# The first two column blocks of each up projection as a fourth group of seven block products, with weight sums added up in DRAM

## What is computed

```python
def squared_relu_mlp(u, w_up, w_down):        # u 512 x 1024, w_up 1024 x 4096, w_down 4096 x 1024
    return jnp.square(jax.nn.relu(u @ w_up)) @ w_down
...
    # layer 0, before its MLP: the chunked scan
    X = (xh * dt[..., None]);  dA = dt * A;  cs = jnp.cumsum(dA, axis=2)
    seg = cs[:, :, :, None] - cs[:, :, None, :]
    Lmat = jnp.exp(jnp.where(causal, seg, -jnp.inf))
    y_diag = jnp.einsum("bclsgr,bcsgrp->bclgrp", CB[..., None] * Lmat, X)
```

## Time and profile before

| | us |
|---|---|
| Median of 3 runs (1261.75 to 1262.09) | 1261.78 |
| Span of the profiled execution, first to last instruction | 1260.5 |
| PE busy | 1252.7 |
| DVE busy | 923.8 |
| ACT busy | 754.1 |
| POOL busy | 168.1 |

### The profile page before, as it was taken

How to read it: one execution, slowest core, us unless ns; L and a number is a source line. 1 busy time by engine, 2 the same in 40 slices (tenths; PEclk the granted TensorE clock), 3 DMA queues, 4 the chain that set the end, 5 groups by cost and what they waited for, 6 DMA issues and landing times.

```text
span 1260.5 us, 19569 instructions
## 1 busy us (share of the span) xinstructions
PE 1252.7 (99%) x7651; PEld 1087.3 (86%) x7651; DVE 923.8 (73%) x1261; ACT 754.1 (60%) x1277; POOL 168.1 (13%) x197
## 2 busy tenths in 40 slices
PE   9999999999999999999999999999999999999998
PEld 8788888888888989999888898788889999988886
DVE  5676786898743686687887974877576776869886
ACT  6655455687653655567565753777554566666563
POOL 0046355473000000000000000000000000000000
PEclk9999999999999999999999999999999999999999
DMA  8488878385663378668676527656626576877554
GB/s 273 154 285 275 237 169 198 111 238 123 176 217 105 128 173 235 216 113 218 190 249 191 193 74 171 131 125 154 169 96 235 113 198 226 174 221 239 188 175 155
DMA packets 110530, 230.29 MB, mean 183 GB/s; under 512 B 8150, under 2 KB 18918, under 8 KB 110182
## 3 DMA queue, kind: packets, MB, share of 16 engines
q1 hardware_dynamic: 84384, 159.93, 38.8%
q0 software_dynamic: 21760, 67.11, 24.6%
q10 hardware_dynamic: 4294, 2.00, 0.8%
HBM read 225.69 MB, written 70.04 MB: 235 GB/s over the span
## 4 chain that ended last, share of the span: by engine, by line
PE 99%; DMA 0%; DVE 0%; ACT 0%; issue 0%; SPq 0%; DVEq 0%; ACTq 0%
PE G L2441 34%; PE G L2949 5%; PE G L2953 5%; PE G L2951 5%; PE X L2912 4%; PE X L2910 4%; PE X L2908 4%; PE X L2464 4%; PE X L2949 3%; PE X L2953 3%; PE X L2951 3%; PE X L2526 3%; PE G L2526 3%; PE G L2912 3%; PE G L2910 3%; PE G L2908 3%
## 5 line engine op out<-in xcount | busy, mean ns | idle before, releaser
L1427 ACT ACTIVATE whi<-raw 128x1024 fp32r<-128x1024 f32 x112 | 118.4, 1059 | 106.7 <-PE G L2953 47.3
L2193 DVE TENSOR_TENSOR wlo<-raw,whi 128x1024 fp32r<-128x1024 f32 x112 | 135.5, 1220 | 48.6 <-ACT whi L1427 48.5
L1627 DVE TENSOR_TENSOR wlo<-raw,whi 128x1024 fp32r<-128x1024 f32 x77 | 94.6, 1228 | 82.8 <-ACT whi L897 82.6
L1345 ACT ACTIVATE whi<-raw 128x1024 fp32r<-128x1024 f32 x84 | 88.8, 1061 | 102.3 <-PE X L2912 52.6
L2441 PE MATMUL G<-uhi,whi 128*128 128x512 f32 x352 | 144.4, 410 | 0.2 <-DVE ulo L1644 0.2
L2126 DVE TENSOR_TENSOR wlo<-raw,whi 128x1024 fp32r<-128x1024 f32 x84 | 102.6, 1222 | 55.8 <-ACT whi L1345 55.3
L2441 PE MATMUL G<-uhi,wlo 128*128 128x512 f32 x352 | 137.7, 391 | 0.0
L2441 PE MATMUL G<-ulo,whi 128*128 128x512 f32 x352 | 137.3, 390 | 0.0
L897 ACT ACTIVATE whi<-raw 128x1024 fp32r<-128x1024 f32 x77 | 81.4, 1057 | 77.8 <-PE G L2441 28.5
L797 POOL DMA_DIRECT2D tsum<-in_w_down x32 | 33.0, 1043 | 572.5 <-PE G L2441 331.5
L842 POOL TENSOR_SCALAR csrow<-csrow,small 128x128 f32<-128x128 f32 x96 | 87.3, 1099 | 1.4 <-DMA csrow<-cs_rows 1.3
(11 more groups left out here) (457 smaller groups left out, 3689.6 us busy)
## 6 DMA issues: line engine op xcount, KB each, us to landing
tsum<-in_w_down POOLq DMA_DIRECT2D x48, 1024.0 KB, 9.9
raw<-in_w_up SPq DMA_DIRECT2D x64, 512.0 KB, 6.2
raw<-tsum SPq DMA_DIRECT2D x64, 512.0 KB, 3.9
raw<-in_w_down SPq DMA_DIRECT2D x48, 512.0 KB, 4.7
raw<-in_ssd_w_out SPq DMA_DIRECT2D x16, 512.0 KB, 4.1
raw<-in_swa_w_in SPq DMA_DIRECT2D x16, 512.0 KB, 4.6
...
```

Of the source, the lines that this page charges most:

```text
L1345: act.activation(whi[n % 4][:, :, :], up_right(g, r, q), ACT.Copy).then_inc(hi_done, up_fill(g, k))
L1427: act.activation(whi[n % 4][:, :, :], down_raw[n % 4][:, :, :], ACT.Copy).then_inc(hi_done, 1)
L1627: dve.tensor_tensor(wlo[q][:, :, :], src[:, :, :], whi[q][:, :, :].bitcast(F32), ALU.subtract).then_inc(lo_done, 1)
L2193: dve.tensor_tensor(wlo[n % 4][:, :, :], down_raw[n % 4][:, :, :], whi[n % 4][:, :, :].bitcast(F32), ALU.subtract).then_inc(lo_done, 1)
```

## The change

The first two column blocks of each up projection become a fourth group of seven block products, in front of the three pairs: F1, F2, F4, F5, F6, F3, F7, two panels each, 14 panels instead of eight. F1 and F2 use tokens 0 to 255, so they stand where the first half of `split` stood; of the last two token tiles only the half of `uhi` and `ulo` that F4 needs is written. ACT keeps three results (`p5_kept`, `u2_kept`, `p4_kept`) and copies F1 into the banks of F6; DVE makes three of the four outputs from them.

The four weight sums of this group are not made by DVE but in DRAM (`usum`), by eight more DMAs of 1 MB per layer from POOL: copy and add in turn, each behind a wait for the one before it. Those of layer 0 stand in the scan, one per unit from unit 8 on. Those of layer 1 stand in the down projection of layer 0, at panels 130, 136, ... 172 (`U1_SUM_AT`). Token sums and `up_add` change signs so that all weight sums are plain; their number in the pairs is unchanged. The tables of the `tsum` DMAs move a few panels later.

```diff
+U1_SUM_AT = tuple(range(130, 178, 6))
+F1, F2, F4, F5, F6, F3, F7 = range(PROD)
...
+            def up_weight_sum(i, n):
+                x, src, op = ((0, 1, None), (0, 2, ALU.add), (2, 2, None), (2, 4, ALU.add),
+                              (1, None, None), (1, 4, ALU.add), (3, None, None), (3, 3, ALU.add))[n]
...
+                if USUM * i + n > 0:
+                    ps.wait_ge(usum_in, 16 * (USUM * i + n))
+                if op is None:
+                    ps.dma_start(usum[i][x], src).then_inc(usum_in, 16)
+                else:
+                    ps.dma_start(usum[i][x], src, accum_op=op).then_inc(usum_in, 16)
...
                 elif v % 2:
                     weight_sum(0, 3 + (v - 8) // 2)
+                if v >= 8:
+                    up_weight_sum(0, v - 8)
...
+                if i == 0:
+                    for n, p in enumerate(U1_SUM_AT):
+                        ps.wait_ge(panel_done, p)
+                        up_weight_sum(1, n)
...
             def mlp(i, f0, blk):
-                split(2 * i, N_F[i], blk, up_half_still, f0)
...
-                gemm(N_F[i] + 1, blk + 1, 4, weights_still(u_of), u_wait(U0[2 * i + 2]), second_free)
+                pe.wait_ge(ulo_ready, U0[m + 2] + 4)
+                pe.wait_ge(og1_done, 4 * m + 2)
+                for t in range(2):
+                    for q in range(2):
+                        if t == 0:
+                            pe.wait_ge(lo_done, 4 * blk + q + 1)
+                        for y in (2 * t, 2 * t + 1):
+                            mm = first_block(F1, q, y, quadrant(0, 0), True, True)
...
+                first_product(F4, quadrant(1, 1), True)
...
+                first_product(F5, up_left(P5), True)
...
+                first_product(F6, up_left(P6), False)
...
+                first_product(F3, up_left(P3), False)
...
+                first_product(F7, up_left(P7), False)
```

507 lines of the change are left out of this document (310 added, 197 removed).

## The result

The changed kernel takes **1275.0 us** (median of 4 executions, 1274.67 to 1275.25), the kernel before 1261.82 (4, 1261.75 to 1262.09). The ratio is 1.0103 with a 95% interval of 1.0091 to 1.0115: 1.0% slower. The forecast was 1263.6 with a range of 1257 to 1269, so it missed by 11.4 us and the time lies outside the range. The profiled execution took 1275.25 with a span of 1273.5, 13.0 more than before.

What follows compares the result with a forecast made beforehand. The prediction took PE, busy 99% of the span, to bound the kernel. Its sum was 1261.78 - 9.02 (fewer matmuls) + 0.4 (F1's wait) + 10.4 (scan) = 1263.6 us, with a range of 1257 to 1269.

Steps and rivals of the forecast that it cites:

- The signs of being wrong that the prediction named: POOL past its unit 12 wait before 261 us, new group over 43 us, or PE waiting in the down projection.
- Fewer matmuls, 9.02 us: Up projection's first two column blocks: fewer matmuls save 4.51 us per layer, 9.02 us for both.
- F1's second half, 0.2 us per layer: New group's start: F1 wants panel 1 earlier and PE waits; 0.2 us per layer, 0.4 us in all.
- F5, "it holds by 0.4 us": New group, F5: panel 6 and token sums are ready near 433.0, wanted at 433.39 us, so no wait.
- six steps: DVE before F5: token sums and panel parts, 1.14 us each, the last ending near 433.0 us.
- Loads, four outputs and three copies: Nothing.: New group: loads, output work and ACT's copies are ready when PE wants them and cost nothing.
- The scan, 10.4 us: Scan, units 12 and 14: POOL waits for DMA landings; PE stands 7.2 us, is 10.4 late, bounds 9.0 and 12.5.
- the scan costs more than 12.5: Rival, scan: half clock plus DVE's and ACT's stalled lists cost more than 12.5 us, 1266 to 1269; chance 0.07.
- The clock: Scan, after PE's wait: half clock could lose PE 3 us, but costs nothing beyond unit 14's 10.4 us.
- The down projection, "I take nothing": Down projection of layer 0: the eight added DMAs make PE wait for nothing; bounds 0 to 4 us.
- The rival: Down projection, panels 130 to 178: layer 1's sums delay loads, four adding DMAs cost about 1 us each, 1267.6; chance 0.12.
- The fit of the Trainium skill: DMA from GpSimd: 2.0 us plus bytes over 436 per ns, 4.4 us for 1 MB; not used in the forecast.

Runs made afterwards that it cites:

- last_loads_early: Changed kernel with the new group's panels 12 and 13 loaded after panel 6's low part instead of panel 9's, on their own semaphores: 1272.4 us.
- tsum76_later: Changed kernel with the `tsum` DMAs of panels 76 and 83 at 81 and 84, and those of 216 and 220 at 221 and 222: 1272.7 us.
- scan_copies: Changed kernel with layer 0's four adding `usum` DMAs made plain copies of the same size: 1271.1 us.
- only_unit12_moved: Changed kernel with only unit 12's `usum` DMA moved from the unit's head to the end of its POOL list: 1274.8 us.
- scan_issue_at_end: Changed kernel with each scan unit's `usum` DMA issued at the end of the unit's POOL list, not at its head: 1270.7 us.
- down_dmas_only: Kernel before plus only layer 1's eight `usum` DMAs in the down projection of layer 0, results unread: 1264.7 us.
- down_copies_only: Kernel before plus eight `usum` DMAs in the down projection of layer 0, all plain copies, results unread: 1262.4 us.

## Why the prediction was wrong, point by point

The signs of being wrong that the prediction named came: both new groups took over 43 us (43.39 and 43.74) and PE waited in the down projection. The steps that failed are the size of the scan's term (3.1 us too small), the landing of loads beside the new DMAs in the down projection (3.6 us, put at nothing), the late loads of the new group and the pairs (3.5 us, put at nothing) and F5's wait (0.9 us in both layers). That is 11.1 of the 11.4 us.

**Fewer matmuls, 9.02 us.** Right. With the charge at F1 the forecast is 42.16 us per group. Where loads are in time a group takes 42.60, in six kernels, and the 0.44 us between are F5's wait.

**F1's second half, 0.2 us per layer.** Right: at 429.3, where F1 goes on to panel 1, PE loses 0.19.

**F5, "it holds by 0.4 us".** Wrong by 0.9, and it cost 0.46 per layer. The token sums started at 441.55, 0.75 later than forecast (427.3 and the 13.5 us of the scan), mostly because ACT's copy of the last tile waits 0.61 us for DVE's `ulo`; I had counted ACT's work and not that wait. The "six steps" of the text are a slip: its list names five, its 433.0 is reckoned with five, and in the run the fifth, the low part of panel 6, ended at 447.3, just before F5. "If it did not, each miss would cost its own size" was right.

**"Loads, four outputs and three copies: Nothing."** Wrong: 0.8 (group 0) + 1.6 (pairs 0) + 1.1 (group 1) = 3.5 us. I looked at whether the sums were in DRAM, not at what SP's order does when the two shared panels hold up eight others. last_loads_early and tsum76_later each bring it back.

**The scan, 10.4 us.** The mechanism was right in place and order; the size was 13.5. Two items: the second landing came 9.1 us behind the first and not 7.0 (a wait of 8.9 instead of 7.2, within the stated 9.3). That moved unit 13's DMAs too, since they are issued behind `Xdec` of unit 12 (278.3 instead of 276.4); from there on the forecast held (17.0 us to the landing against 17.3), so unit 14 was 12.4 us late and not 10.4. Then came 1.1 for row blocks, which I had priced in no term. The upper bound of 12.5 was too low, "the scan costs more than 12.5" had a chance of 0.07, and it is what happened, though not by the half clock that this rival names.

**The clock.** That the half clock would cost nothing beyond unit 14's lateness was right for this kernel: PE still stood 1.2 us at unit 14 after it. That rests on the second wait being there; in scan_copies and only_unit12_moved nothing hid the half clock, and it cost 2.6 and 1.5 us. The 4.6 to 5.6 us that the prediction read from the end of the trace before the clock was down are no guide to a wait inside the kernel: here it was down about 2 us after the last matmul, and in tsum76_later behind a wait of 2.1 us. In scan_issue_at_end a wait of 2.3 us in the down projection left it at 1.00.

**The down projection, "I take nothing".** Wrong: 3.6 us. The rival had it: place, mechanism (the loads land later; medians in 590 to 745 us are 5.3 us for `tsum` and 6.9 for `w_down` panels against 4.0 and 4.5) and size (+4) are as written, with a chance of 0.12. The argument against it, that such DMAs stand every four panels beside the pairs without a wait, compared two stages with different room: beside the pairs of the kernel before the share is 0.73 with those DMAs in it (461 to 582 us), while the down projection has 0.67 without any and 0.86 with them in down_dmas_only. The rival's finer point, that adding costs and not copying, holds on the kernel before (down_copies_only).

**The fit of the Trainium skill** ("DMA: Bandwidth & Descriptors", on a DMA from GpSimd, 4.4 us for 1 MB). It was rightly not used: here a plain copy of 1 MB between the loads took 7.2 us to land (median, down_copies_only), an adding one 11.5 to 12.4 (down_dmas_only), and in units 11 and 13 one issued right behind another 13.9 (a copy) to 19.2 (adding).

**The range.** The bounds of the likeliest case come out of its own terms as 1262.2 to 1265.7, not 1262.0 to 1265.8, which changes nothing. The two tails (scan above 12.5, down projection +4) were given chances as if only one could come. Both have to do with DMAs, the adding ones above all, that land later or hold loads up more than the rows before showed; that this is one common cause is argued and not shown. Both came: 1263.6 and the 3.1 and 3.6 us are 1270.3, above the 1269 of the range even without the 3.5 us of the late loads.
